# Five subtractions of 128x2048 numbers moved from VectorE to GpSimd between the stages of a two-block network

## The reference

```
def swiglu(h, w_gate, w_up, w_down):
    return (jax.nn.silu(h @ w_gate) * (h @ w_up)) @ w_down

for layer in range(DEPTH_2):
    g = g_norm[layer]
    f = swiglu(rms_norm_2(x, g[0]), w_ffn_gate[layer, 0], w_ffn_up[layer, 0], w_ffn_down[layer, 0])
    x = x + 0.5 * rms_norm_2(f, g[1])
    h = rms_norm_2(x, g[2])
    ...                     # layer 0: short_conv_mixer;  layer 1: diff_attention with shared k, v
    x = x + rms_norm_2(m, g[3])
    f = swiglu(rms_norm_2(x, g[4]), w_ffn_gate[layer, 1], w_ffn_up[layer, 1], w_ffn_down[layer, 1])
    x = x + 0.5 * rms_norm_2(f, g[5])
    if layer == N_A_LAYERS - 1:
        k, v = shared_kv(x, g_kv, w_kv)
```

## Time and profile before

| | |
|---|---|
| median of three runs | 2022.16 us (2021.72 to 2024.08) |
| the profiled execution | 2018.27 us, of which the span of instructions is 2016.4 us |
| TensorE busy | 92% of the span |
| VectorE busy | 66% |
| ScalarE busy | 40% |
| GpSimd busy | 21%, nearly all of it while it gathers experts in the first block |
| mean granted TensorE clock | 0.969 of full speed |

### The profile page before, as it was taken

The page is one execution under the profiler, slowest core; times in us unless marked ns, Lnnn a source line. Parts: engine busy times, 40 slices in busy tenths (PEclk is TensorE's granted clock), DMA queues, the critical chain, the costliest instruction groups (busy, mean ns, idle before and its releaser), DMA issues.

```text
span 2016.4 us, 28023 instructions
## 1 busy us (share of the span) xinstructions
PE 1846.1 (92%) x9758; PEld 1411.3 (70%) x9758; DVE 1326.7 (66%) x2588; ACT 814.3 (40%) x1375; POOL 413.5 (21%) x523
## 2 busy tenths in 40 slices
PE   7999999987878877878889999999999999999998
PEld 7989899833333333333368888988879888878887
DVE  5556856777778767777656567665565555776555
ACT  4456244222222222222244455454455544665443
POOL 4000000355554655555510000000000000010000
PEclk9999999998988988889999999999999999999999
DMA  8333266699999999999966564555554656435552
GB/s 238 101 99 111 71 171 169 258 417 422 422 422 422 422 421 422 421 422 422 422 232 208 187 209 155 177 189 188 187 188 157 203 189 210 148 109 165 188 188 102
DMA packets 224243, 496.66 MB, mean 246 GB/s; under 512 B 21653, under 2 KB 170278, under 8 KB 191398
## 3 DMA queue, kind: packets, MB, share of 16 engines
q1 hardware_dynamic: 181264, 221.36, 34.8%
q0 software_dynamic: 38224, 273.04, 32.8%
q10 hardware_dynamic: 4678, 1.21, 0.3%
HBM read 494.53 MB, written 1.05 MB: 246 GB/s over the span
## 4 chain that ended last, share of the span: by engine, by line
PE 69%; DMA 13%; DVE 7%; issue 4%; POOL 3%; ACT 3%; DVEq 0%; POOLq 0%; ACTq 0%
PE ps L2210 41%; PE acc L2210 26%; DMA arena<-in_peer_uv,idx_now 8%; DMA rows_x<-in_peer_uv,idx_now 4%; DMA rows_lo<-in_peer_uv,idx_now 1%; POOL rows L731 1%; DVE lo L1402 1%; DVE spare_lo L1918 0%; POOL arena L727 0%; POOL rows_lo L731 0%; ACT spare_hi L1123 0%; POOL idx_now L724 0%; POOL rstd L646 0%; DVE x L2024 0%; ACT hi L789 0%
## 5 line engine op out<-in xcount | busy, mean ns | idle before, releaser
L2210 PE MATMUL ps<-xboth,hi 128*128 128x512 f32 (+2 forms) x2400 | 653.7, 346 | 2.6 <-DVE xboth L1423 2.1
L1402 DVE TENSOR_TENSOR lo<-raw,hi 128x2048 fp32r<-128x2048 f32 x198 | 451.6, 2283 | 197.9 <-ACT hi L789 197.9
L2210 PE MATMUL ps<-xboth,lo 128*128 128x256 f32 x1840 | 492.2, 282 | 0.0
L2210 PEld LDWEIGHTS ps<-xboth,hi 128*128 128x128 f32 (+1 forms) x2400 | 407.2, 190 | 50.0 <-issue 4.3
L789 ACT ACTIVATE hi<-raw 128x2048 fp32r<-128x2048 f32 x198 | 376.3, 1902 | 24.3 <-PE acc L2210 16.2
L2210 PEld LDWEIGHTS ps<-xboth,lo 128*128 128x128 f32 x1840 | 348.9, 190 | 14.4
L641 POOL TENSOR_SCALAR ss<-ss 128x1 f32<-128x1 f32 x28 | 9.4, 337 | 1005.3 <-ACT arena L1185 850.5
L2210 PE MATMUL acc<-rows,diag 128*128 128x512 f32 x192 | 117.4, 776 | 77.6 <-ACT diag L1093 75.9
L2210 PE MATMUL acc<-arena,diag 128*128 128x512 f32 x384 | 172.7, 595 | 6.2 <-ACT diag L1093 5.7
L2210 PEld LDWEIGHTS acc<-rows,diag 128*128 128x128 f32 x192 | 46.8, 252 | 147.4 <-issue 131.2
L2210 PEld LDWEIGHTS acc<-arena,diag 128*128 128x128 f32 x384 | 72.0, 190 | 100.3 <-issue 83.9
(11 more groups left out here) (407 smaller groups left out, 3083.3 us busy)
## 6 DMA issues: line engine op xcount, KB each, us to landing
raw<-in_w_ffn_gate SPq DMA_DIRECT2D x44, 1024.0 KB, 5.3
raw<-in_w_ffn_down SPq DMA_DIRECT2D x44, 1024.0 KB, 5.1
raw<-in_w_ffn_up SPq DMA_DIRECT2D x41, 1024.0 KB, 5.3
raw<-in_w_in SPq DMA_DIRECT2D x29, 1024.0 KB, 5.4
raw<-in_w_conv_in SPq DMA_DIRECT2D x11, 1024.0 KB, 5.3
raw<-in_w_kv SPq DMA_DIRECT2D x6, 1024.0 KB, 5.7
raw<-in_w_out SPq DMA_DIRECT2D x4, 1024.0 KB, 5.2
raw<-in_w_conv_out SPq DMA_DIRECT2D x4, 1024.0 KB, 6.7
```

The source lines that it names most:

```text
L1402: v.tensor_tensor(lo[s][:, 0:WORDS[p]], raw[s][:, 0:WORDS[p]], hi[s][:, 0:WORDS[p]].bitcast(F32), ALU.subtract).then_inc(lo_done, 1)
L2210: return nc.tensor.matmul(out, l, r, start=first, stop=last)
```

## The change

`split_spare` gets a second version in the GpSimd program. Five of the seven calls on VectorE go: those for conv_in, kv and q in the last step of a feed-forward stage, that for ffn1 after the convolution, and that for ffn2 in the kv stage. The calls for ffn0 and ffn3 stay on VectorE. The operation, its operands and its semaphores are the same.

```
+            def split_spare(s):
+                pool.wait_ge(spare_hi_done, s + 1)
+                g.tensor_tensor(spare_lo, spare_raw, spare_hi.bitcast(F32), ALU.subtract).then_inc(spare_lo_done, 1)
+
-            def post(name):
+            def post(name, spare=None):
                 load_gain(name)
+                if spare:
+                    split_spare(SPARE[spare])
                 after = dict(POSTS)[name]
...
-            post("p0")
-            post("pc")
-            post("p1")
-            post("p2")
+            post("p0", "conv_in")
+            post("pc", "ffn1")
+            post("p1", "kv")
+            split_spare(SPARE["ffn2"])
+            post("p2", "q")
...
                 split(p0 + 4, 3, i - 1)
-                if following is not None:
-                    split_spare(following)
                 product(p0 + 2, i, 3, i - 1)
...
             peeled(dve, 4, conv)
-            split_spare(SPARE["ffn1"])
...
             split(p0 + 4)
-            split_spare(SPARE["ffn2"])
             split(p0 + 5)
```

## The result

The changed kernel took 2033.37 us (median of 4 runs, 2031.35 to 2037.12), the kernel before 2022.35 us (4 runs, 2021.72 to 2024.08). The ratio is 1.0061, 95% interval 1.0049 to 1.0073: 11.0 us slower where 7.3 were forecast, on the side and in the range (2021 to 2035) that the prediction gave.

A forecast was written before the change was run, and what follows sets the result against it. TensorE, 92% busy, was taken as the bound, waiting behind the spare subtractions. Three feed-forward shifts of +1.64 us and +2.37 at the conv end, kv nothing, sum to +7.3 on 2022.16: 2029.5 us, range 2021 to 2035.

The forecast's parts named there:

- What bounds the kernel, and the five places: TensorE, 92% busy, bounds; the subtraction matters at ends of ffn0, ffn1, ffn2 and conv, not in the kv stage.
- How long GpSimd takes: GpSimd's subtraction of 2048 columns was put at 4.5 us, between bounds of 1.8 and 5.8 us.
- Whom it holds: A VectorE instruction with two SBUF inputs waits out GpSimd's whole reading instruction; one with at most one runs freely.
- the PSUM instruction: Feed-forward ends: the product's first instruction, reading PSUM, runs freely; rival has it held too, +9.4 us, 2031.6, chance 0.08.
- The shifts: With GpSimd's duration d: d - 2.86 (+1.64 us) at three feed-forward ends, d - 2.13 (+2.37) at the conv end.
- The sum, 7.3 us: Three feed-forward shifts and the conv shift, 4d - 10.7, give +7.3 us with d = 4.5.
- the prediction's own last sign: The prediction is wrong if the granted clock falls behind TensorE's grown gaps.
- the rival that had it: Clock falls behind up to four TensorE gaps of 3.2 to 3.4 us: +10 on top, to 2039.5, chance 0.07.
- the 2.5 that was worked out from the earlier trace: Clock loss of about 2.5 us behind a 6.75 us TensorE gap, from stretches at 0.50 and 0.78 of full clock.
- The relief alone, 2.4 us: VectorE freed of the subtractions, nothing added: 2.04 us at three feed-forward ends plus 0.41 at the conv end.

The follow-up runs named there:

- r2_write_only: Changed kernel with GpSimd writing zeros for about as long, reading nothing, in place of each of the five subtractions; 2018.7 us, ratio 0.9990.
- r5_half: Changed kernel with GpSimd subtracting only the first 1024 of the 2048 columns; 2019.59 us, ratio 0.9994.
- r4_warm: Changed kernel with ten extra products, results unused, in each of TensorE's four long gaps; 2027.52 us, ratio 1.0037.
- the second: The changed kernel run once more, unedited, on another chip, against the kernel before; 2034.73 us, ratio 1.0071.
- r1_relief: Changed kernel with GpSimd only writing 16 columns in place of each of the five subtractions; 2018.67 us, ratio 0.9987.
- r7_early_pool: Changed kernel with ScalarE's spare high halves one place earlier in the last feed-forward step and ffn1's subtraction back on VectorE; 2019.5 us, ratio 0.9996.
- r3_pieces: Changed kernel with each GpSimd subtraction cut into four of 512 columns; 2022.28 us, ratio 1.0010.
- r6_early: Kernel before, with both spare halves made one place earlier on ScalarE and VectorE at the ends of ffn0, ffn1 and ffn2; 2018.93 us, ratio 0.9992.
- r8_best: Kernel before, with the earlier spare halves at three feed-forward ends and ScalarE's spare high half earlier at the conv end; 2017.06 us, ratio 0.9983.

## Why the prediction was right, and where it fell short

- **What bounds the kernel, and the five places.** Right. The gaps grew at four places and not in the kv stage, and the ledger has it so.
- **How long GpSimd takes.** 4.5 was taken, 4.58 measured. From the rows alone 4.5 was a choice between bounds of 1.8 and 5.8 us, and that it came so close is luck as far as they go. The Trainium skill's 4497 ns for an fp32 add of 2048 columns (GPSIMD Engine Reference, section 3.1) is 2% below what the trace shows.
- **Whom it holds.** Right, with the PSUM instruction free: beside GpSimd's subtraction a VectorE instruction with one SBUF input runs freely (L1976, 0.69 us), one with two is held (L1980, 2.94), and beside a write-only GpSimd instruction the one with two runs freely as well (r2_write_only, 0.69). The Trainium skill (SBUF — State Buffer, Who interferes with whom) has a VectorE instruction with two SBUF inputs contend with a GpSimd instruction that reads SBUF, but not with one that only writes it. These traces agree.
- **The shifts.** +1.64 at a feed-forward end, 1.57 measured by the gap; +2.37 at the conv end, 2.32 measured. Two small errors cancel here: with d = 4.58 the sum would give +1.72 and +2.45, but a held instruction needs 0.14 us less after the hold than the sum has it (r5_half), and the handover to GpSimd is 0.08 us instead of 0.10.
- **The sum, 7.3 us.** It is what r4_warm measured, 7.1, with the clock kept up. The term that was mis-sized is the clock, and by the prediction's own last sign ("or if the granted clock falls behind them") it was wrong there. The forecast set it at nothing, and the rival that had it got a chance of 0.07, with the argument that 3.2 us is half of the 6.75 us gap in the earlier trace rows. That was no argument: none of the rows that I read had a gap between 1.6 and 6.75 us followed by a look at the clock. It fell behind two of four gaps in one trace and three of four in the other, at 1.6 to 2.7 us each; the 2.5 that was worked out from the earlier trace rows is at the upper end. By medians it is 3.9 us in the first comparison (11.0 less 7.1) and 7.2 in the second. That the first result lay within the range is in part luck: the second, 14.3 us above before, is more than the 12.8 that the upper end of the range allows.
- **The relief alone, 2.4 us.** r1_relief found 1.8, with 2.4 inside its interval, and its landmarks give 2.3.

## What to carry to other kernels

Before work is moved to GpSimd, look at what VectorE does during its time: in these traces an instruction of VectorE with both inputs in SBUF waits for the end of a GpSimd instruction that reads SBUF, so on a critical chain the price follows GpSimd's duration (d less 2.86 or 2.13 us here) and not VectorE's saving. If it must run there, start it in VectorE's slack (r7_early_pool) or cut it into pieces (r3_pieces). Here neither was faster than leaving the work on VectorE in a better place (r6_early, r8_best). And when a wait on TensorE grows, here from 1.58 to 3.15 us, add a fall of the clock to the sum as a term with a price and a chance of its own. A run with the gaps filled by products whose results are not used shows how much of the loss it is.

## What the runs showed of the hardware

- GpSimd's f32 subtraction with a rounded output: 4.58 us for 2048 columns, 2.40 for 1024, 1.29 for 512. Behind a VectorE instruction it counts the wait in its own duration (4.93, 3.34 us).
- A held VectorE instruction ends 0.14 us sooner after the hold than its own duration would have it (0.55 of 0.69 us, 2.15 of 2.29).
- With work queued on both, the engines alternated instruction by instruction (r3_pieces: 1307.69, 1309.84 and 1311.00 are the ends of a piece, a split and a piece).
- Behind TensorE gaps of 3.15 to 3.85 us the granted clock fell to half in some executions and not in others, sometimes from the first product on (0.77 us), sometimes 1.1 us later. Once, in r3_pieces, it fell behind gaps of 1.58 and 0.79 us that the other traces have as well, there at full clock. What decides it is open.
